# Expert weights in 48 loads ordered by job, phase and side

## What is computed

```python
for e in range(N_EXPERTS):                       # 16
    h = jax.nn.silu(x @ w1[e]) * (x @ w3[e])     # 1024 -> 512, twice
    out = out + gates[:, e:e + 1] * (h @ w2[e])  # 512 -> 1024
```

## Time and profile before

| | us |
|---|---|
| median of 3 runs | 2518.15 |
| lowest and highest | 2515.71, 2518.84 |
| the profiled execution | 2521.37 |
| its span | 2519.5 |
| first to last product of the job loop | 579.86 to 914.70 |

### The profile page before, as it was taken

How to read it: one execution, slowest core, us unless ns; L and a number is a source line. 1 busy time by engine, 2 the same in 40 slices (tenths; PEclk the granted TensorE clock), 3 DMA queues, 4 the chain that set the end, 5 groups by cost and what they waited for, 6 DMA issues and landing times.

```text
span 2519.5 us, 28945 instructions
## 1 busy us (share of the span) xinstructions
PE 2358.8 (94%) x10176; PEld 1657.1 (66%) x10177; DVE 970.0 (39%) x1756; ACT 522.3 (21%) x1097; POOL 133.3 (5%) x150
## 2 busy tenths in 40 slices
PE   6999999977689889899999999899999999999999
PEld 2564456643234348668888888476675778888888
DVE  7331267552000032553434433334333354335521
ACT  2300046531111133442111100111212202111100
POOL 1000044400001010000000000000000000000000
PEclk9999999887899999989999999899999999999999
DMA  9301124256977972112222222131121122322220
GB/s 337 130 10 51 33 74 186 107 210 238 386 264 269 329 300 64 38 34 68 84 84 87 87 68 100 68 101 58 41 96 56 56 67 86 92 90 84 84 103 31
DMA packets 81185, 299.24 MB, mean 119 GB/s; under 512 B 9024, under 2 KB 9024, under 8 KB 80464
## 3 DMA queue, kind: packets, MB, share of 16 engines
q1 hardware_dynamic: 75312, 272.14, 31.1%
q0 software_dynamic: 5792, 26.00, 2.8%
HBM read 283.94 MB, written 14.16 MB: 118 GB/s over the span
## 4 chain that ended last, share of the span: by engine, by line
PE 86%; DVE 6%; ACT 3%; issue 2%; DMA 2%; SPq 2%; DVEq 0%; POOL 0%; ACTq 0%; POOLq 0%
PE products L1523 39%; PE products L954 7%; PE products L1353 7%; PE products L1133 6%; PE products L1428 3%; PE products L1371 3%; PE products L1670 2%; PE products L1184 2%; PE products L1605 2%; PE products L1040 1%; PE products L1262 1%; PE products L1478 1%; PE products L1087 1%; PE products L1097 1%; PE products L1197 1%
## 5 line engine op out<-in xcount | busy, mean ns | idle before, releaser
L1523 PE MATMUL products<-normed,weights_and_work 128*128 128x264 f32 (+1 forms) x1520 | 347.7, 384 | 0.0
L1523 PEld LDWEIGHTS products<-normed,weights_and_work 128*128 128x128 f32 x1520 | 288.5, 190 | 49.2 <-issue 3.4
L1766 ACT ACTIVATE weights_and_work<-products 128x256 f32<-128x256 f32 (+4 forms) x243 | 108.9, 466 | 602.7 <-PE products L1523 156.4
L1353 PE MATMUL products<-weights_and_work 128*64 128x512 f32 x768 | 180.7, 631 | 48.7 <-DMA weights_and_work<-in_experts 48.0
L1523 PE MATMUL products<-weights_and_work,mixed 128*128 128x256 f32 (+1 forms) x800 | 182.3, 382 | 0.8 <-ACT weights_and_work L1766 0.8
L1353 PEld LDWEIGHTS products<-weights_and_work 128*64 128x64 f32 x768 | 65.4, 146 | 162.3 <-issue 160.7
L1523 PEld LDWEIGHTS products<-weights_and_work,mixed 128*128 128x128 f32 x800 | 151.8, 190 | 24.4 <-ACT weights_and_work L1766 1.6
L1133 PE MATMUL products<-weights_and_work,normed 128*128 128x512 f32 x352 | 154.8, 601 | 8.4 <-DVE normed L2176 8.4
L1523 PE MATMUL products<-weights_and_work 128*128 128x256 f32 (+1 forms) x672 | 151.0, 385 | 8.2 <-DVE residual L3061 5.2
L1523 PE MATMUL products<-weights_and_work,normed 128*128 128x264 f32 (+1 forms) x704 | 155.6, 382 | 0.0
L1523 PE MATMUL products<-normed,mixed 128*128 128x264 f32 (+1 forms) x672 | 154.1, 382 | 0.0
(11 more groups left out here) (518 smaller groups left out, 2912.6 us busy)
## 6 DMA issues: line engine op xcount, KB each, us to landing
weights_and_work<-in_weights SPq DMA_DIRECT2D x303, 512.0 KB, 4.3
weights_and_work<-in_experts SPq DMA_DIRECT2D x192, 512.0 KB, 5.5
results<-normed SPq DMA_DIRECT2D x8, 512.0 KB, 6.9
residual<-in_x POOLq DMA_DIRECT2D x1, 2048.0 KB, 16.5
weights_and_work<-in_dft_half POOLq DMA_DIRECT2D x1, 2048.0 KB, 8.5
token_rows<-mixed SPq DMA_DIRECT2D x4, 512.0 KB, 3.1
normed<-results SPq DMA_DIRECT2D x4, 512.0 KB, 6.8
mixed<-results SPq DMA_DIRECT2D x4, 512.0 KB, 7.4
```

What stands on the lines that cost most here:

```text
L1353: m = pe.matmul(ps[UNIT * b:UNIT * (b + 1), side, :], job_t[:, k, UNIT * b:UNIT * (b + 1)], expert_w[b][:, s, at:at + 512], start=(k == 0) ...
L1523: m = pe.matmul(bank(p, n), left(k), right(k), start=(fresh and k == 0), stop=(k == kt - 1), skip_group_check=True)
L1766: act.activation(out, src, ACT.Copy, scale=scale).then_inc(bank_free[p.bank], 1)
```

## The change

The loads of experts become 48 loads of four tiles: an expert has three phases (`w1`, `w3`, `w2`). They are ordered by first job, then phase, then side, so that where both sides change at one job their loads alternate by phase. Load n uses the landing semaphores of lane n mod 3, four of them to a lane, twelve in all as before; its transfers wait for those of load n - 3. On SP the loop runs 14 times over three loads each, with one `value_load` for the turn, two for each load and one for each tile. On PE a job reads nine landing counts (three phases by three lanes) where it read one, and waits for three semaphores ahead of a tile. The landing counts and the load table are worked out on DVE with the job (or load) number along the partitions, turned into one partition by nine and six small products on PE, and copied out; `jobs_ready` now comes after the copy of the landing counts. The first six loads, ahead of the jobs, are also ordered by phase.

```diff
+PHASES, PHASE_TILES = 3, 4
+LOADS = 16 * PHASES
+LANES = 3
...
@@ SP
-            with sp.Fori(2, EXPERTS) as it:
-                e = sp.value_load(order_i[0:1, bass.ds(it, 1)], min_val=0, max_val=EXPERTS - 1)
-                landed_by = sp.value_load(landed_i[0:1, bass.ds(it, 1)], min_val=0, max_val=16 * EXPERTS)
-                to = sp.value_load(buffer_i[0:1, bass.ds(it, 1)], min_val=0, max_val=RING * TILE)
-                for i, s in enumerate(slots):
-                    passed_by = sp.value_load(after_i[0:1, i, bass.ds(it, 1)], min_val=1, max_val=MAX_JOBS * EXPERT_TILES)
-                    sp.wait_ge(e_passed, passed_by)
-                    sp.wait_ge(e_landed[s], landed_by)
-                    sp.dma_start(weights_and_work[:, bass.ds(to + s * TILE, TILE)], d["experts"][e, i]).then_inc(e_landed[s], 16)
+            with sp.Fori(2 * PHASES // LANES, LOADS // LANES) as it:
+                landed_by = sp.value_load(landed_i[0:1, bass.ds(it, 1)], min_val=0, max_val=16 * LOADS)
+                for n in range(LANES):
+                    at = bass.ds(it * LANES + n, 1)
+                    part = sp.value_load(loads_i[0:1, 0, at], min_val=0, max_val=LOADS - 1)
+                    to = sp.value_load(loads_i[0:1, 1, at], min_val=0, max_val=(2 * RING - PHASE_TILES) * TILE)
+                    for i in range(PHASE_TILES):
+                        lane_in = e_landed[n * PHASE_TILES + i]
+                        passed_by = sp.value_load(loads_i[0:1, 2 + i, at], min_val=1, max_val=MAX_JOBS * EXPERT_TILES)
+                        sp.wait_ge(e_passed, passed_by)
+                        sp.wait_ge(lane_in, landed_by)
+                        sp.dma_start(weights_and_work[:, bass.ds(to + i * TILE, TILE)], by_phase[part, i]).then_inc(lane_in, 16)
...
@@ PE, ranks(): new, ahead of the jobs
+                for n, (p, columns, count) in enumerate(((r["landings"], landing_col, LANES * PHASES), (r["loads"], load_col, 6))):
+                    fill(p)
+                    pe.wait_ge(columns_set, n + 1)
+                    for v in range(count):
+                        m = pe.matmul(ps[0:1, p.bank, 48 * v:48 * (v + 1)], columns[:, v:v + 1], ident[:, 0:48], start=True, stop=True)
+                    finish(p, m)
...
@@ PE, experts()
-                    landing = pe.value_load(landing_i[0:1, bass.ds(it, 1)], min_val=16, max_val=16 * EXPERTS)
+                    landing = [[pe.value_load(landing_i[0:1, PHASES * n + phase, bass.ds(it, 1)], min_val=16, max_val=16 * LOADS)
+                                for n in range(LANES)] for phase in range(PHASES)]
+
+                    def tile_in(phase, i):
+                        for n in range(LANES):
+                            pe.wait_ge(e_landed[n * PHASE_TILES + i], landing[phase][n])
...
-                            pe.wait_ge(e_landed[s], landing)
+                            tile_in(side, pair)
...
@@ DVE, router(): between lines 2566 and 2581
+                link(tt_(sooner_t, bcast(first, 1, EXPERTS), bcast(first, 2, EXPERTS), ALU.is_lt))
+                link(dve.tensor_reduce(sooner, sooner_t, AX_X, ALU.add))
+                link(tt_(same_t, bcast(first, 1, EXPERTS), bcast(first, 2, EXPERTS), ALU.is_equal))
+                link(dve.tensor_reduce(same, same_t, AX_X, ALU.add))
...
+                ts(landing_col, landing_col, 1.0, 16.0, ALU.max, ALU.mult).then_inc(columns_set, 1)
+                dve.wait_ge(columns_set, 1)
...
+                link(ts(load_hot, load_no, partition, None, ALU.is_equal))
+                for v, of in enumerate((load_ids, buffer_e, after_e)):
+                    link(tt_(load_t, load_hot, of, ALU.mult))
+                    link(dve.tensor_reduce(load_col[:, v:v + 1], load_t.rearrange("p g e -> p (g e)"), AX_X, ALU.add))
...
+                dve.tensor_copy(landing_i[0:1].rearrange("p g j -> p (g j)"), ps[0:1, p.bank, 0:48 * LANES * PHASES]).then_inc(bank_free[p.bank], 1)
                 dve.tensor_copy(last_i, last_f)
                 dve.tensor_copy(n_jobs_i, count[:, 0:1]).then_inc(jobs_ready, 1)
```

More of the change, by code:

```diff
@@ L247, in plan @@
     r["slots"], = b.many(1)
-    r["ms_meta"], = b.many(1)
+    r["ms_meta"], r["landings"], r["loads"] = b.many(3)
     r["before_jobs"] = b.settle()
@@ L528, in two_blocks @@
         result_f, slot_t = arena[:, 13760:13760 + JOBS], arena[:, 13790:13790 + JOBS]
[L529 to L537, removed]
+        same_t, sooner_t = piece(arena, 14000, EXPERTS, EXPERTS), piece(arena, 14260, EXPERTS, EXPERTS)
+        sooner, first, same, within, load_base = (arena[:, a:a + EXPERTS] for a in range(15640, 15720, EXPERTS))
+        load_no, landing_e = piece(arena, 15720, PHASES, EXPERTS), piece(arena, 15768, PHASES, EXPERTS)
+        begun_e, load_t, load_hot = arena[:, 15816:15832], piece(arena, 15832, PHASES, EXPERTS), piece(arena, 15880, PHASES, EXPERTS)
+        after_e, buffer_e = piece(arena, 15928, PHASES, EXPERTS), piece(arena, 15976, PHASES, EXPERTS)
+        load_col, last_load = arena[:, 16024:16030], arena[:, 16030:16033]
+        landing_col = arena[:, 14540:14540 + LANES * PHASES]
+        landed_i_f = arena[:, 16292:16292 + LOADS]
+        load_ids = piece(arena, 16040, PHASES, EXPERTS)
+        landing_i = piece(arena, 19040, LANES * PHASES, 48).bitcast(I32)
+        loads_i = piece(arena, 17644, 6, 48).bitcast(I32)
+        landed_i = arena[:, 18028:18028 + LOADS].bitcast(I32)
         gather_f = arena[:, 18470:18470 + JOBS]
@@ L776, in _, with first_of @@
             slots = [(before + i) % RING for i in range(EXPERT_TILES)]
[L778 to L789, removed]
-            ready(sp, r["OT", ST - 1][1])
[L791 to L795, removed]
+            by_phase = d["experts"].rearrange("e (g i) p t -> (e g) i p t", g=PHASES)
+            def first_of(n):
+                phase, e = n // 2, n % 2
+                for i in range(PHASE_TILES):
+                    s = slots[PHASE_TILES * phase + i]
+                    lane_in = e_landed[n % LANES * PHASE_TILES + i]
+                    if n >= LANES:
+                        sp.wait_ge(lane_in, 16 * (n // LANES))
+                    if e == 0 and phase < 2:
+                        sem_, value = read_by(before + PHASE_TILES * phase + i - RING)
+                        sp.wait_ge(sem_, value)
+                    elif e == 0:
+                        ready(sp, r["w_out"][2 * i + 1])
+                    sp.dma_start(expert_w[e][:, s, :], by_phase[PHASES * e + phase, i]).then_inc(lane_in, 16)
+            first_of(0)
+            ready(sp, r["OT", ST - 1][1])
+            for n in range(1, 2 * PHASES):
+                first_of(n)
             for t in range(ST):
@@ L1365, in experts @@
                         s = slots[8 + k]
-                        pe.wait_ge(e_landed[s], landing)
+                        tile_in(2, k)
                         if k % 2 == 0:
@@ L2567, in router @@
                 read(dve, p)
[L2568 to L2573, removed]
@@ L2574, in router @@
-                link(tt_(over, over, bcast(landing_e, 1, JOBS), ALU.mult))
-                link(dve.tensor_reduce(landing_f, over, AX_X, ALU.max))
+                link(stt(first, side, -UNIT / 2.0, key, ALU.mult, ALU.add))
+                link(ts(first, first, 1.0 / UNIT, None, ALU.mult))
+                ids = lane[:, 0:EXPERTS].rearrange(by_buffer, b=2)
+                link(tt_(sooner_t, bcast(first, 1, EXPERTS), bcast(first, 2, EXPERTS), ALU.is_lt))
+                link(dve.tensor_reduce(sooner, sooner_t, AX_X, ALU.add))
@@ new lines, in router @@
+                link(tt_(same_t, bcast(first, 1, EXPERTS), bcast(first, 2, EXPERTS), ALU.is_equal))
+                link(dve.tensor_reduce(same, same_t, AX_X, ALU.add))
+                link(stt(within, same, -1.0, side, ALU.add, ALU.mult))
+                link(stt(load_base, sooner, float(PHASES), within, ALU.mult, ALU.add))
+                for phase in range(PHASES):
+                    ins = stt(load_no[:, phase], same, float(phase), load_base, ALU.mult, ALU.add)
+                link(ins)
@@ new lines, in router @@
+                link(ts(begun_e, first, partition, None, ALU.is_le))
+                link(tt_(load_t, load_no, bcast(begun_e, 1, PHASES), ALU.mult))
+                link(dve.tensor_reduce(last_load, load_t, AX_X, ALU.max))
+                for n in range(LANES):
+                    ins = ts(landing_col[:, PHASES * n:PHASES * (n + 1)], last_load, float(LANES - 1 - n), 1.0 / LANES, ALU.add, ALU.mult)
+                link(ins)
+                link(ts(landing_col, landing_col, ROUND, None, ALU.add))
@@ new lines, in router @@
+                link(ts(landing_col, landing_col, ROUND, None, ALU.subtract))
+                ts(landing_col, landing_col, 1.0, 16.0, ALU.max, ALU.mult).then_inc(columns_set, 1)
+                dve.wait_ge(columns_set, 1)
+                for phase in range(PHASES):
```

(12 more changed lines are left out.)

14 lines of the change are left out of this document (8 added, 6 removed).

## The result

The changed kernel takes 2558.35 us (median of 4 runs, 2552.8 to 2558.95) against 2518.49 us for the one before: a ratio of 1.0154, 95% interval 1.0137 to 1.0172. It is 39.9 us slower; 39 were forecast. The profiled execution is the fastest of the four, 2552.8 us; the other three took 2557.85 to 2558.95.

What follows compares the result with a forecast made beforehand. Expert-weight landings were taken to bound PE's products, behind SP's ordered loads. Terms - 58.8 + 38.5 + 31.9 + 9.4 + 18 = + 39.0 us on 2518.15 gave 2557 us, range 2528 to 2571.

Steps and rivals of the forecast that it cites:

- The table's making: DVE's work before job 0: jobs_ready 4.5 us later, first product 9.4 us later with the first table loads, once.
- The signs named ahead of the run: PE rests 3 to 4 us at borders, then half clock; jobs 1, 5, 10 unwaiting; job 0 near 589.
- Minus 58.8 us for the landing waits: Expert products on PE: interleaved loads can win 48.0 us of landing waits plus 10.8 us of slower tiles, partly given back.
- Table loads on PE, 3.5 us a border: Top of PE's job loop: nine table loads outlast the queued products, 3.5 us at each of 11 borders, 38.5 us.
- The clock, 2.9 us a job: PE's tiles after each border: the rest brings half clock, 2.9 us at each of 11, 31.9 us.
- SP, job 4 at 134.8 us after job 0: SP's load issue for jobs 1 to 3: job 4 starts at 724, not PE's 705.4; 18 us taken.
- A: PE at job borders: the clock stays up through rests of 3.5 us; plus 16 us, 2534 us; chance 0.22.
- B: PE's queue at the job loop's top covers the table loads; minus 6 us, 2512 us; chance 0.09.
- C: Jobs 5 and 10 still wait, as three-lane waits hold PE for loads not yet needed; 2573 us; chance 0.05.
- D: SP's new loop: index arithmetic adds 0.06 us to each of 19 loads a turn, 7 us; 2564 us; no separate chance.

Runs made afterwards that it cites:

- e7: The kernel of e4 with its 48 loads ordered by job, side and phase instead of job, phase and side: 2521.05 us, ratio 1.0005.
- e4: The changed kernel with PE reading three landing counts ahead of each phase and SP one pass count for each load: 2485.47 us, ratio 0.9864.
- e6: The changed kernel with its 48 loads ordered by job, side and phase instead of job, phase and side: 2567.88 us, ratio 1.0193.
- e1: The kernel before, with PE's one landing-count table load made nine times at the top of each job: 2546.18 us, ratio 1.0107.
- e2: The changed kernel, with PE reading three landing counts just ahead of each phase's tiles instead of nine at the job's top: 2523.83 us, ratio 1.002.
- e5: The changed kernel, with unused products issued ahead of each of the last five table loads at the top of a job: 2544.12 us, ratio 1.0103.
- e3: The changed kernel, with SP reading one pass count for each load of four tiles and adding 0 to 3 in the wait: 2528.08 us, ratio 1.004.

## Why the prediction was right, and where its terms were off

The forecast was 2557 us and 39 us slower. In the two profiled executions the steps can be told apart. The table's making and the first nine loads moved the first product from 579.86 to 584.93 although the work ahead of it ended 5.6 us sooner, + 10.7 us; the job loop took 360.6 us in place of 334.8, + 25.8 us; the rest of the kernel 0.6 us. Together + 37.1 us. The signs named ahead of the run came as said (rests for issue, half clock at the start of each job, jobs 1, 5 and 10 without a landing wait, SP's turn near 20 us), but for jobs 2 and 3, which also wait 6.52 and 6.02 us ahead of their first tile.

- **Minus 58.8 us for the landing waits**: as said at jobs 1, 5 and 10, which begin without one. e7 against e4 gives the interleaving 35.6 us where nothing else binds; most of the rest is the loads of jobs 1 to 3, with the DMA engines full from job 2 to 3 (411 GB/s): in e4 job 4 begins 115.5 us after job 0, 22 us more than four jobs and the slow start of job 0 need. In the changed kernel the interleaving itself was worth only 9.5 us (e6), since table loads that run while PE waits for a landing cost nothing, and without that wait they cost their rest.
- **Table loads on PE, 3.5 us a border**: mechanism right (e1, e2), size mostly 3.0 to 3.1 us of rest and 3.2 a job, by 0.76 us a load. One thing was left out. Where the job before ended on late tiles (712.08 to 720.86), PE had few products queued to hide behind: the loads began 1.9 us ahead of the end of its products (718.9), at 838.22 4.1 us ahead, and the rest was 5.7 us (at 726.58).
- **The clock, 2.9 us a job**: mechanism right (e5), size wrong. From job 4 on the tiles took 1.3 to 1.7 us longer, and 2.8 once (job 6). At 838.22 the slow stretch was short (0.50 from 838.70 to 842.00, 1.00 from 842.20 on). I had taken the upper price of the earlier trace rows for the reason that the lower ones followed the longest rests; the rows do not bear that out, as the rest of 8.11 us, the shortest, was followed by tiles of 15.47 us, only 1.5 more. Jobs 4 to 11 came 27.8 us apart in place of 29.1, so the sum held 9 us too much.
- **SP, job 4 at 134.8 us after job 0**: mechanism right (e3), 141.65 us measured. The turn of 20.1 us was 20.26, 1.5 us over the 72 tiles; the last tiles took 7 us to land, not 5, their products came later still, and the border after them cost 5.7 us. 7 us too little.
- **The table's making, 9.4 us**: 10.7. `jobs_ready` came 4.5 us later, as forecast (566.05 to 575.00, 8.95 us, in place of 571.65 to 576.06, 4.41 us). What I missed is a wait for free banks: PE is held at line 1347 for 2.2 us, until 576.3, because DVE empties the load table's bank only with the copy at 575.84, which ends at 576.28. Of the 2.2 us some 1.2 lie behind `jobs_ready`, set at 575.1; that is about what the term was short of.

The four errors are - 9, + 7, + 1.3 and about - 2 us (the last job's tiles were slow by 1.3 us, not 2.9), so they nearly cancel; the total was better than its parts, and that was luck. So is the last step to 39.9 us: the executions that can be compared give 37.1, and the other 2.8 lie in how single executions differ.

Of the rivals, A (the clock stays up) did not happen in the changed kernel; e5 shows about what it would have given, 14 us less, where A's sum had 23. B needed more cover than the 20 products in the queue; e1 shows that it is not there. The Trainium skill gives TensorE's queue as 64 deep (TensorE: Matmul & The Clock Gate, Architectural detail). Taken as 32 products with their weight loads, as in rival B, that would have left a rest of 0.7 us; this case's trace does not agree, with rests of 3.0 to 3.6 us, as the lead of 4.4 us in the earlier trace rows said. C (jobs 5 and 10 still wait) is false for the changed kernel, but came true in e2 for another reason: once PE's borders were short, SP was late. D: the added index arithmetic cost at most the 0.16 us by which SP's turn is over the forecast.

## What to carry to other kernels

Count what a sequencer does between two stretches of its engine's work. A table load into a register is hidden as long as it is shorter than the work already queued for the engine (some 4 us here). When several stand together at a border, what goes beyond that is rest, and here the clock fell after it: put them in small groups, each just ahead of its use. And where a queue of transfers is read in order, one register and an added constant can replace a load for each transfer; here the good order of the loads was worth 9.5 us with both sequencers burdened and 35.6 us with both relieved.

## What the runs showed of the hardware that was not expected

- Rests of 3.0 to 3.6 us on PE, in a loop in which it is otherwise full, were followed by the half clock (0.50) at each of the eight borders that had them in the changed kernel's profiled run; rests of 2.0 to 2.1 us at four of six (e1). With the rest filled the clock stayed at 1.00 (e5).
- After rests of 3.0 to 3.6 us the half clock cost the eight tiles 1.3 to 1.7 us, and 2.8 once; after rests of 8.1 to 8.4 us in the earlier trace rows it cost 1.5 to 2.9.
- The same work can meet or miss a slow stretch of 13 us far from the change (at 473 us, after a rest of 1.9 us in both kernels), and that is 5.6 us of the time.
